# Mixture of experts on one core: the order of the second projections within a pair of experts

## What is computed

```python
logits = (xt @ router).astype(jnp.float32)
top_v, top_i = lax.top_k(logits, MOE_TOP_K)            # 2 of 8
top_w = jax.nn.softmax(top_v, axis=-1)
gates = jnp.sum(jax.nn.one_hot(top_i, N_EXPERTS) * top_w[..., None], axis=1)
for e in range(N_EXPERTS):
    gate, up = jnp.split(xt @ w_in[e], 2, axis=-1)     # w_in[e]: 1024 x 7168
    out = out + gates[:, e:e + 1] * ((jax.nn.silu(gate) * up) @ w_out[e])   # w_out[e]: 3584 x 1024
```

## Time and profile before

| | |
|---|---|
| median of 3 runs | 1430.3 us (1427.23 to 1434.27) |
| the profiled execution | 1427.71 us, its span 1426.0 us |
| TensorE busy | 1392.5 us, 98% of the span |
| VectorE busy | 1132.3 us, 79% |
| ScalarE busy | 959.8 us, 67% |
| low halves in `wlo` and `wlo_more` (VectorE, L1032) | 2259 to 2288 ns each |
| high halves (ScalarE, L876) | 1918 to 1920 ns each |
| HBM read | 444.63 MB |

### The profile page before, as it was taken

The page is one execution under the profiler, slowest core; times in us unless marked ns, Lnnn a source line. Parts: engine busy times, 40 slices in busy tenths (PEclk is TensorE's granted clock), DMA queues, the critical chain, the costliest instruction groups (busy, mean ns, idle before and its releaser), DMA issues.

```text
span 1426.0 us, 18557 instructions
## 1 busy us (share of the span) xinstructions
PE 1392.5 (98%) x7394; PEld 1182.6 (83%) x7394; DVE 1132.3 (79%) x791; ACT 959.8 (67%) x798; POOL 55.2 (4%) x64
## 2 busy tenths in 40 slices
PE   9999999999999999999999999999999999999995
PEld 9987789999979888888788788788788788787784
DVE  4456655454465678998999998999988999999996
ACT  5334544433454458797888797888787887787874
POOL 1002200000000003002000002000000000000000
PEclk9999999999999999999999999999999999999998
DMA  9654546555554329999999999999999999999990
GB/s 358 233 172 151 199 157 213 198 178 178 195 188 155 141 89 387 420 395 405 400 419 420 385 378 418 386 418 420 394 372 419 390 417 420 392 399 421 416 406 32
DMA packets 158743, 446.89 MB, mean 313 GB/s; under 512 B 7088, under 2 KB 46000, under 8 KB 158656
## 3 DMA queue, kind: packets, MB, share of 16 engines
q1 hardware_dynamic: 156832, 439.38, 80.5%
q0 software_dynamic: 1824, 6.33, 1.3%
HBM read 444.63 MB, written 1.05 MB: 313 GB/s over the span
## 4 chain that ended last, share of the span: by engine, by line
PE 68%; DVE 25%; issue 3%; ACT 3%; POOL 0%; DVEq 0%; ACTq 0%; POOLq 0%
PE ps L1504 20%; PE ps L1506 20%; PE ps L1505 20%; DVE wlo L1032 13%; DVE wlo_more L1032 6%; ACT whi L876 2%; PE ps L1980 2%; DVE gT_lo L1032 1%; DVE act L1400 1%; PE ps L1841 1%; DVE h L1391 1%; PE ps L1942 1%; PE ps L1943 1%; PE ps L1550 1%; DVE wlo L418 1%
## 5 line engine op out<-in xcount | busy, mean ns | idle before, releaser
L1032 DVE TENSOR_TENSOR wlo<-raw,whi 128x2048 fp32r<-128x2048 f32 (+1 forms) x214 | 479.1, 2259 | 33.5 <-ACT whi L876 32.8
L876 ACT ACTIVATE whi<-raw 128x2048 fp32r<-128x2048 f32 x208 | 395.7, 1918 | 107.4 <-PE ps L1506 100.7
L418 DVE TENSOR_TENSOR wlo<-raw,whi 128x2048 fp32r<-128x2048 f32 x80 | 183.6, 2294 | 155.3 <-ACT whi L411 155.3
L411 ACT ACTIVATE whi<-raw 128x2048 fp32r<-128x2048 f32 x82 | 156.8, 1912 | 153.2 <-PE ps L1506 149.7
L1504 PE MATMUL ps<-xT_hi,whi 128*128 128x256 f32 x576 | 163.3, 284 | 0.0
L1506 PE MATMUL ps<-xT_hi,wlo 128*128 128x256 f32 x576 | 163.0, 283 | 0.0
L1505 PE MATMUL ps<-xT_lo,whi 128*128 128x256 f32 x576 | 163.0, 283 | 0.0
L1504 PE MATMUL ps<-whi,xg_big 128*128 128x512 f32 x336 | 135.1, 402 | 3.4 <-DVE wlo L1032 3.4
L1942 PE MATMUL ps<-whi,xg_small 128*128 128x512 f32 x336 | 135.0, 402 | 2.7 <-DVE wlo L1032 1.8
L1506 PE MATMUL ps<-whi,xg_big 128*128 128x512 f32 x336 | 132.0, 393 | 0.0
L1505 PE MATMUL ps<-wlo,xg_big 128*128 128x512 f32 x336 | 131.5, 391 | 0.0
(11 more groups left out here) (269 smaller groups left out, 2686.5 us busy)
## 6 DMA issues: line engine op xcount, KB each, us to landing
raw<-in_moe_w_in SPq DMA_DIRECT2D x168, 1024.0 KB, 8.6
raw<-in_moe_w_out SPq DMA_DIRECT2D x84, 1024.0 KB, 7.8
more_raw<-in_moe_w_in SPq DMA_DIRECT2D x56, 1024.0 KB, 8.4
more_raw<-in_moe_w_out SPq DMA_DIRECT2D x28, 1024.0 KB, 8.2
raw<-in_ret_w_in SPq DMA_DIRECT2D x23, 1024.0 KB, 7.1
raw<-in_ffn_w_in SPq DMA_DIRECT2D x22, 1024.0 KB, 4.9
raw<-in_ffn_w_out SPq DMA_DIRECT2D x11, 1024.0 KB, 4.9
raw<-in_ret_w_out SPq DMA_DIRECT2D x8, 1024.0 KB, 4.9
```

What stands on the lines that cost most here:

```text
L411: nc.scalar.activation(whi[:, u % SPLIT, :], src, ACT.Copy).then_inc(hi_done, 1)
L418: nc.vector.tensor_tensor(wlo[:, u % SPLIT, :], src, whi[:, u % SPLIT, :].bitcast(F32), ALU.subtract).then_inc(lo_done, 1)
L876: nc.scalar.activation(moe_split(n)[0], moe_raw(n), ACT.Copy).then_inc(hi_done, 1)
L1032: return nc.vector.tensor_tensor(dst, src, hi.bitcast(F32), ALU.subtract)
```

## The change

Within a pair, the small expert's outs (of its previous block) now stand in the big expert's phase, between big gate and big up, and the big expert's outs (of the same block) stand in the small expert's phase, between small gate and small up. In the last block of a pair the big outs stand behind small gate and small up. So at most four units of one expert stand in a row within a block. The big expert's outs come one phase after its ups, where they used to come in its next block. In the last block of the last pair only two of the small expert's third-block outs stand between big gate and big up; the other two and its last two are at the end.

The steps of the drains follow. The turns of a big block are now at one and three units after its last up (before: two and three), their low halves at two and four. The small high half is at two units after the last up unit (before: three), the small low half at three (before: five). The gathers keep their distances from the starts of their phases; the start of a small phase is now its gate behind the big ups. The small experts' y is drained one unit later. The turned hidden values of the very first block go to banks 2 and 3 as in the others, and the last big expert's second scatter goes to banks 2 and 3 and doesn't wait for the first one's sum.

```diff
--- before.py
+++ after.py
@@ -84,15 +84,20 @@
 
     LAST = len(BLOCK_UNITS) - 1
     STREAM, START = [], {}
-    for phase in range(JOBS * (LAST + 1)):
-        pair, b, j = phase // (2 * (LAST + 1)), phase // 2 % (LAST + 1), 2 * (phase // (2 * (LAST + 1))) + phase % 2
-        START[j, b] = len(STREAM)
-        if phase == JOBS * (LAST + 1) - 1:
-            STREAM += units_of(j, "gate", b) + units_of(j, "up", b) + units_of(j - 1, "out", b)
-            STREAM += units_of(j, "out", b - 1) + units_of(j, "out", b)
-        else:
-            before_out = [] if j < 2 and b == 0 else units_of(j, "out", b - 1) if b else units_of(j - 2, "out", LAST)
-            STREAM += units_of(j, "gate", b) + before_out + units_of(j, "up", b)
+    for pair in range(JOBS // 2):
+        for b in range(LAST + 1):
+            big, small = 2 * pair, 2 * pair + 1
+            end = pair == JOBS // 2 - 1 and b == LAST
+            START[big, b] = len(STREAM)
+            small_out = units_of(small, "out", b - 1) if b else units_of(small - 2, "out", LAST) if pair else []
+            STREAM += units_of(big, "gate", b) + small_out[:2 if end else None] + units_of(big, "up", b)
+            START[small, b] = len(STREAM)
+            if b < LAST:
+                STREAM += units_of(small, "gate", b) + units_of(big, "out", b) + units_of(small, "up", b)
+            else:
+                STREAM += units_of(small, "gate", b) + units_of(small, "up", b) + units_of(big, "out", b)
+            if end:
+                STREAM += small_out[2:] + units_of(small, "out", b)
     END = {(j, part, b): n for n, (j, part, b, q) in enumerate(STREAM)}
     assert len(STREAM) == len(set(STREAM)) == JOBS * JOB_UNITS
 
@@ -101,22 +106,23 @@
     BIG_HALVES = [(j, b, half) for j, b in BIG_BLOCKS for half in range(BLOCK_UNITS[b] // 2)]
     SILU_AT = {END[j, "gate", b] + half: (j, b, half) for j, b, half in BIG_HALVES}
     MUL_AT = {END[j, "up", b] + half: (j, b, half) for j, b, half in BIG_HALVES}
-    TURN_AT = {END[j, "up", b] + 2 + half: (j, b, half) for j, b, half in BIG_HALVES}
-    LO_AT = {END[j, "up", b] + 3 + half: (j, b, half) for j, b, half in BIG_HALVES}
+    TURN_AT = {END[j, "up", b] + 1 + 2 * half: (j, b, half) for j, b, half in BIG_HALVES}
+    LO_AT = {END[j, "up", b] + 2 + 2 * half: (j, b, half) for j, b, half in BIG_HALVES}
     GATE_AT = {END[j, "gate", b]: (j, b) for j, b in SMALL_BLOCKS}
     GATE_TURN_AT = {END[j, "gate", b] + 2: (j, b) for j, b in SMALL_BLOCKS}
     UP_AT = {END[j, "up", b]: (j, b) for j, b in SMALL_BLOCKS}
     UP_TURN_AT = {END[j, "up", b] + 1: (j, b) for j, b in SMALL_BLOCKS}
     SMALL_MUL_AT = {END[j, "up", b] + 2: (j, b) for j, b in SMALL_BLOCKS}
-    SMALL_HI_AT = {END[j, "up", b] + 3: (j, b) for j, b in SMALL_BLOCKS}
-    SMALL_LO_AT = {END[j, "up", b] + 5: (j, b) for j, b in SMALL_BLOCKS}
+    SMALL_HI_AT = {END[j, "up", b] + 2: (j, b) for j, b in SMALL_BLOCKS}
+    SMALL_LO_AT = {END[j, "up", b] + 3: (j, b) for j, b in SMALL_BLOCKS}
     GATHER_AT = {START[j, b] + i: (pair, k) for pair in range(1, JOBS // 2)
                  for k, (j, b, i) in enumerate([(2 * pair - 2, 1, 5), (2 * pair - 2, 1, 7), (2 * pair - 2, 1, 9),
                                                 (2 * pair - 1, 1, 5), (2 * pair - 1, 1, 7), (2 * pair - 1, 1, 9),
                                                 (2 * pair - 2, 2, 5), (2 * pair - 2, 2, 7)])}
     SEL_AT = {START[j - j % 2, 2] + 1 + 3 * (j % 2): j for j in range(JOBS)}
-    Y_AT = {END[j, "out", LAST]: j for j in range(JOBS - 1)}
-    SCATTER_AT = {END[j, "out", LAST] + (4 + 4 * t if j < JOBS - 2 else 3 + 3 * t): (j, t) for j in range(JOBS - 1) for t in range(T)}
+    Y_AT = {END[j, "out", LAST] + j % 2: j for j in range(JOBS - 1)}
+    SCATTER_AT = {END[j, "out", LAST] + (4 + 4 * t if SMALL[j] else 3 + 3 * t): (j, t) for j in range(JOBS - 2) for t in range(T)}
+    SCATTER_AT.update({END[JOBS - 2, "out", LAST] + 3 + t: (JOBS - 2, t) for t in range(T)})
     ADD_AT = {n + 1: jt for n, jt in SCATTER_AT.items()}
     FIRST_GATHER = 5
     assert len(GATHER_AT) == KD * (JOBS // 2 - 1) and max(ADD_AT) == len(STREAM) and max(SMALL_LO_AT) < len(STREAM)
@@ -474,9 +480,11 @@
 
         def turn_bank(j, b, half):
 
-            if j == 0 and b == 0:
-                return 4 + half
             return 3 if b == LAST else 2 + half
+
+        def scatter_bank(j, t):
+
+            return 2 if j == JOBS - 2 and t == 1 else 4 + 2 * (j % 2)
 
         def sel_of(j):
             return sel[:, j // 2 % 2, :, j % 2 * P:(j % 2 + 1) * P]
@@ -1457,7 +1465,7 @@
                     j, t = ADD_AT[n]
                     at = 1 + POSITION[j]
                     dve.wait_ge(h_scaled, T)
-                    add_scattered(T * j, t, gate_of[:, t, at:at + 1], at=4 + 2 * (j % 2))
+                    add_scattered(T * j, t, gate_of[:, t, at:at + 1], at=scatter_bank(j, t))
                 big_drains(n)
                 small_drains(n)
                 moe_lo(n + MSPLIT)
@@ -1953,7 +1961,7 @@
                     elif gathered_by(START[j, b]):
                         pe.wait_ge(small_copied, gathered_by(START[j, b]))
                 if q == 0 and part == "up":
-                    if b == LAST or j == 1 and b == 0:
+                    if b == LAST:
                         pe.wait_ge(big_mul, halves(j, b))
                     else:
                         pe.wait_ge(big_lo, halves(j, b))
@@ -2021,9 +2029,9 @@
                     j, t = SCATTER_AT[n]
                     pe.wait_ge(selT_ready, j + 1)
                     pe.wait_ge(y_lo_done, 2 * j + 2)
-                    if t == 1:
+                    if t == 1 and j < JOBS - 2:
                         pe.wait_ge(summed, T * j + 1)
-                    scatter(t, selT[j % 2], y_hi[j // 2 % 2], y_lo[j // 2 % 2], 4 + 2 * (j % 2))
+                    scatter(t, selT[j % 2], y_hi[j // 2 % 2], y_lo[j // 2 % 2], scatter_bank(j, t))
                 if n in SEL_AT:
                     j = SEL_AT[n]
                     if SMALL[j]:
```

## The result

The changed kernel takes **1457.3 us** (median of 4 runs, 1456.57 to 1458.31), the kernel before 1429.4 beside it: a ratio of 1.0195, interval 1.018 to 1.0211. The profiled executions stand 28.9 us apart (1456.57 and 1427.71). The change makes the kernel 2% slower.

What follows compares the result with a forecast made beforehand. TensorE, 98% busy, was taken as the bound, with memory near but not waited for. Terms of -17.8, -1.1, +20.6, +8.1 and +6.8 made +16.6 on 1427.7, so 1444.3; with the runs' median 2.6 higher, forecast 1447 us, range 1434 to 1458.

Steps and rivals of the forecast that it cites:

- pacing rival: VectorE keeps pacing the runs of small units, so half of the 17.8 us stays: 1456 us, chance 0.10.
- The old stalls: TensorE's waits for VectorE in rows of small units: all 17.8 us gained, bounds 9 and 17.8.
- The small low half: Before the third block's small outs, TensorE waits for VectorE's low half of small hidden rows: 4 x 5.15 = 20.6 us lost.
- The gathers: First gather of big blocks two and three waits for both silus, in three pairs: 6 x 1.35 = 8.1 us lost.
- The clock: TensorE's clock falls behind each of the four 5.15 us stalls: 4 x 1.7 = 6.8 us lost, bounds 0 and 14.
- The tail: Last units of the kernel: one stall of 2.35 us instead of 3.4, 1.1 us gained.
- faster rival: Third block's small hidden low half is ready when the second gate unit ends: 1419.5 us, chance 0.05.
- memory rival: Memory sets the pace, so evening out the runs moves nothing: 1430 us, chance 0.05.

Runs made afterwards that it cites:

- split3: Changed kernel with the edits of split, turn and gather together: 1409.2 us, ratio 0.9852 to the kernel before.
- split: Changed kernel with two of the third block's big outs kept back, placed in the fourth block between big gate and the small outs: 1431.0 us.
- queue: Changed kernel, same stream, with the small expert's product, high half and low half of the hidden rows one step earlier, except the very last block: 1442.5 us.
- warm: Changed kernel with 18 small identity matmuls before each of the four waits for the third block's small low half: 1452.8 us.
- turn: Changed kernel with the first hidden turn of a big block one unit later, two units behind its last up: 1447.4 us.
- gather: Changed kernel with the big blocks' gathers one unit later: 1451.7 us.
- queue3: Changed kernel with the edits of queue, turn and gather together: 1425.8 us.
- order: Changed kernel with the fourth block reordered, so that two more big up units stand before the third block's small outs: 1434.5 us.
- all3: Changed kernel with the edits of order, turn and gather together: 1422.0 us, ratio 0.9951 to the kernel before.

## Why the prediction was right, and where it was short

The direction and the deciding mechanism were right, and 1457.3 lies inside the range, 0.7 us below its upper end. That it does is in part luck: the upper end was set for the pacing rival, in which half of the old waits stay. None stayed, and what filled the room is a wait that stands in no term. Of the 28.9 us I had 16.6. By its steps:

- **The old stalls, 17.8 us gained:** right. No wait for a low half of weights is left on TensorE, and split3's pair of 215.0 us confirms the size.
- **The small low half, 4 x 5.15:** right to the hundredth (5.14), and its reason is shown twice, by split (more cover) and by queue (another place in the order).
- **The gathers, 6 x 1.35 = 8.1:** 7.5, since with the overlap of 0.16 the wait is 1.37 us in the second block but 1.12 in the third.
- **The clock, 4 x 1.7 = 6.8:** right that each stall brings a fall, and warm shows that it is the idling; mis-sized, 9.6. The rule of the Trainium skill that I weighed ("TensorE: Matmul & The Clock Gate", HAM oscillation: each burst behind a long wait starts at the low clock) agrees with this trace, four times of four at 4.99 us of idle, and four of four in turn and in gather; at 2.08 us it was two of four in queue and in queue3.
- **The tail:** 1.0 gained, 1.1 said; the idle of 2.30 us stood where the walk had put 2.35. The 0.9 us that the clock gave back in the last scatter stands in no step.
- **The failed step** is in the old stalls' walk, which has the two hidden turns as "some 2.8 us more of TensorE's work" and ends on "Cost nothing". It counts them as cover for VectorE and never asks what they wait for. The change sets the first turn one unit behind the last up, a small one of 1.82 us, where two had stood, and the turn needs VectorE's product, which stands behind the low half of the unit three further on. The prediction's own step lengths would have shown it (an estimate): from the end of the unit before the last up, low half 4.47, less the overlap of 0.09, product 0.68, signal 0.05, in all 5.11 us, against 2.73 + 1.82 = 4.55 of cover, 0.56 us short in each of 16 blocks. It measured **11.3 us** in sum; the run called turn shows it. With the measured terms in the sum the forecast would have been 1459 to 1460.
- The faster rival decided at a stall of 2.7 us each; it was 5.14 and a fall of the clock. Against the pacing rival and the memory rival speak the lists of waits, in which neither wlo nor a DMA stands before a matmul.

## What to carry to other kernels

When units are reordered, count for each moved consumer how many units of cover stand between its producer's start and itself, and look up behind which other instruction the producer is queued: an operation of 0.7 us cost 5.1 because it stood behind a split that could only begin when the unit before the consumer had ended. Do it for every consumer whose distance shrinks, the short ones too: the four long waits cost 20.6 us, the sixteen short ones 11.3. Then walk the chain with the engine's backlog at that moment; here that added 1.5 us to the turns, and 1 us to the idle in each of queue's four places. The finer interleaving was right and worth 1.5% (split3); it needed two units of cover at one place, and the turns and gathers one unit later.

## What I had not expected of the hardware

After an idle of the same length the clock can be down at once, down later or not at all. Behind 2.72 us of idle at the end the kernel before came back slow; the changed kernel came back at full speed and fell after four matmuls (0.49, 0.40, 0.39, 0.40, then 0.57 and 0.63 us). Behind 2.08 us (queue) two places were slow, one from the first matmul and one from the fourth, and two were not. Behind the 2.3 us before the last two units the matmuls were slow in four traces (order, all3, warm, queue3) and not in the seven others that have this wait. Behind 5 us they were slow in all twelve places of the changed kernel, turn and gather. A slow stretch lasted 7 to 14 matmuls of 128 x 512 and cost 1.6 to 2.9 us. So an idle of 2 to 3 us brought a fall only in some places of these runs and one of 5 us in every place, and the price of a fall was fixed in neither.
